# First layer of a two-layer block in float32 on one core: the norm's factor applied after the products instead of before them

## The reference, cut to what matters

```python
def rmsnorm(x, g):
    xf = x.astype(jnp.float32)
    y = xf * lax.rsqrt(jnp.mean(xf * xf, axis=-1, keepdims=True) + RMS_EPS)
    return (y * g.astype(jnp.float32)).astype(x.dtype)

h = rmsnorm(x, norm_mix_pre[l])
proj = h @ w_in[l]
xr, yr, q, k, v, g_rnn, g_attn = jnp.split(proj, IN_OFFSETS, axis=-1)
xr = causal_depthwise_conv(xr, conv_w[l], conv_b[l])
xr = rg_lru(xr, positions, w_a, b_a, w_x, b_x, lam)
y_rnn = xr * jax.nn.gelu(yr)
q, k = rope(q, positions), rope(k, positions)
y_att = sliding_window_sink_attention(q, k, v, attn_sinks[l])
mix = sigmoid(g_rnn) * (y_rnn @ w_rnn_proj[l]) + sigmoid(g_attn) * (y_att @ w_attn_proj[l])
x = x + rmsnorm(mix @ w_out[l], norm_mix_post[l])
...   # an MLP, then a second layer with three kinds of attention and a larger MLP
```

## Time and profile before

| | |
|---|---|
| median of 3 runs | 2827.66 us (2826.63 to 2828.91) |
| the profiled execution | 2828.23 us |
| its span in the trace | 2826.4 us |
| PE busy | 2758.0 us, 98% of the span |
| DVE, ACT busy | 1948.1 us (69%), 1337.4 us (47%) |
| PE waits: for the sum of squares, at the start | 13.4 us |
| PE waits: for normalised tiles (L600) | 8.2 us, 7 times |
| PE waits: for ACT in RG (L740) | 3.3 us, once |

### The profile page before, as it was taken

One profiled execution on the slowest core, in us unless ns is written; L12 is line 12 of the kernel. 1 busy time (PEld: TensorE's weight loads), 2 busy tenths in 40 slices (PEclk: granted clock), 3 DMA queues, 4 the chain that ended last, 5 costly groups with the idle time before them and its releaser, 6 DMA issues.

```text
span 2826.4 us, 50296 instructions
## 1 busy us (share of the span) xinstructions
PE 2758.0 (98%) x16433; PEld 2407.7 (85%) x16433; DVE 1948.1 (69%) x3013; ACT 1337.4 (47%) x2135; POOL 109.7 (4%) x206
## 2 busy tenths in 40 slices
PE   7999999999999999999999999999999999999998
PEld 6888888888887888888888789788888888888887
DVE  7878867766657774457754654856788885688855
ACT  5655455554444443334444443644554444444443
POOL 0000000000010000000000010100110000000000
PEclk9999999999999999999999999999999999999999
DMA  4555544445553556666555354354445545555554
GB/s 174 179 178 176 194 152 154 156 167 185 188 193 126 186 179 229 206 202 213 204 193 195 147 195 152 132 180 143 155 164 188 183 175 196 193 185 186 184 174 163
DMA packets 83196, 503.32 MB, mean 178 GB/s; under 512 B 9685, under 2 KB 17925, under 8 KB 31515
## 3 DMA queue, kind: packets, MB, share of 16 engines
q1 hardware_dynamic: 79868, 491.04, 49.8%
q0 software_dynamic: 3120, 11.14, 1.4%
q10 hardware_dynamic: 144, 0.30, 0.0%
HBM read 500.29 MB, written 10.55 MB: 181 GB/s over the span
## 4 chain that ended last, share of the span: by engine, by line
PE 59%; DVE 5%; issue 3%; ACT 2%; DVEq 0%; ACTq 0%
PE PS L568 33%; PE PS L572 17%; ACT w L1125 1%; PE PS L688 1%; PE PS L689 1%; PE PS L690 1%; PE PS L583 1%; DVE tmp L1713 1%; DVE w L1702 1%; PE PS L585 1%; PE PS L584 1%; DVE tmp L2147 0%; PE PS L875 0%; DVE tmp L2146 0%; PE PS L715 0%
## 5 line engine op out<-in xcount | busy, mean ns | idle before, releaser
L1702 DVE TENSOR_TENSOR w<-w_raw,w 128x1024 fp32r<-128x1024 f32 (+1 forms) x964 | 1099.8, 1173 | 421.1 <-ACT w L1125 419.6
L1125 ACT ACTIVATE w<-w_raw 128x1024 fp32r<-128x1024 f32 (+1 forms) x964 | 942.0, 1009 | 388.9 <-PE PS L572 239.0
L568 PE MATMUL PS<-h,w 128*128 128x512 f32 x3008 | 766.9, 397 | 4.7 <-ACT w L1125 2.1
L568 PEld LDWEIGHTS PS<-h,w 128*128 128x128 f32 x3008 | 540.5, 188 | 120.0 <-issue 18.1
L568 PE MATMUL PS<-u,w 128*128 128x512 f32 x1728 | 442.0, 394 | 5.2 <-ACT w L1125 5.2
L572 PEld LDWEIGHTS PS<-h,w 128*128 128x128 f32 x3008 | 410.1, 190 | 30.1
L572 PE MATMUL PS<-h,w 128*128 128x256 f32 x3008 | 418.7, 282 | 0.0
L568 PEld LDWEIGHTS PS<-u,w 128*128 128x128 f32 x1728 | 308.9, 189 | 58.5 <-ACT w L1125 5.8
L568 PE MATMUL PS<-f,w 128*128 128x512 f32 x1408 | 354.5, 394 | 4.0 <-DVE x L2388 4.0
L568 PEld LDWEIGHTS PS<-f,w 128*128 128x128 f32 x1408 | 254.4, 190 | 49.8 <-DVE x L2388 4.2
L572 PEld LDWEIGHTS PS<-u,w 128*128 128x128 f32 x1728 | 241.5, 190 | 21.0
(11 more groups left out here) (326 smaller groups left out, 2608.7 us busy)
## 6 DMA issues: line engine op xcount, KB each, us to landing
w_raw<-in_w_FU SPq DMA_DIRECT2D x88, 1024.0 KB, 4.7
w_raw<-in_w_UP SPq DMA_DIRECT2D x64, 1024.0 KB, 4.8
w_raw<-in_w_DN SPq DMA_DIRECT2D x64, 1024.0 KB, 4.8
w_raw<-in_w_FD SPq DMA_DIRECT2D x64, 704.0 KB, 4.0
w_raw<-in_w_G SPq DMA_DIRECT2D x32, 1024.0 KB, 4.7
w_raw<-in_w_Q SPq DMA_DIRECT2D x18, 1024.0 KB, 4.7
w_raw<-in_w_X SPq DMA_DIRECT2D x16, 1024.0 KB, 4.8
w_raw<-in_w_Y SPq DMA_DIRECT2D x16, 1024.0 KB, 4.7
```

The source lines that it names most:

```text
L568: pe.matmul(PS[:, bank, :], w_hi[:, 2 * s + hf, k * P:(k + 1) * P], rhs[:, k0 + k].rearrange("p a b -> p (a b)"), start=start and k == 0, ...
L1125: act.activation(w_hi[:, 2 * s + hf, 0:n * P], w_raw[:, s, off * P:(off + n) * P], ACT.Copy)\
L1702: tt(w_lo[:, slot, 0:n * P], w_raw[:, s, off * P:(off + n) * P], w_hi[:, slot, 0:n * P].bitcast(F32), ALU.subtract).then_inc(lo_ready, 1)
```

## The change

The first layer's products no longer take the normalised activations. `h_hi`/`h_lo` are made from x times the gain (`raw_high` on ACT, `raw_lower` on DVE), as each slice of x lands. SP loads the first two slices of x, then both first units of weights, then the other two slices. The squares, their sum, the root and the reciprocal still happen, but later: PE sums them in the middle of unit 2 (`x_sums`), together with two products that give the same sums with tokens along the partitions (for V). The factor is kept in `rstd_x` and later `rstd_g`. It is multiplied

- in X into every merged tile: `merge_x` becomes a copy of the bank's upper half on ACT (`x_lower`), an addition on DVE (`join_halves`) and a product on DVE (`scale_x`), and only then comes `tap`. The taps 2, 1 and 0 of a tile are done in the body of the next unit;
- in Q into `cos` and `sin`, once;
- in Y into every tile (`y_lower`, `join_y`, `scale_y` in place of `merge_y`);
- in V by the scale operand of the copy on ACT;
- for the gates by 16 products of two tiles each in MR and MA (`scale_gates`).

ACT's bodies of phase X are written out instead of being a hardware loop.

```diff
             for name, n, subs in STREAM:
+                if name == "X":
+                    for s in range(2):
+                        sp.dma_start(w_raw[:, s, :], dram["w_X"][s]).then_inc(w_landed[s], 16)
+                    load_x(2)
+                    load_x(3)
+                    sp.wait_ge(lo_ready, 4 + 3)
+                    load(name, 1, n // 2, subs)
+                    continue
...
-            sum_features(0)
-            pe.wait_ge(hi_ready, 1)
-            keep_busy(10, w_hi[:, 0, 0:P], w_hi[:, 0, 0:2 * S])
-            product("X", 16, h2, ready=(h_ready, 4), joint=True)
+            def x_sums(i, s):
+                if isinstance(i, int) and s == 0:
+                    sum_features(0)
+
+            pe.wait_ge(raw_lo, 1)
+            keep_busy(12, h_hi[:, 0, 0:P], h2[:, 0].rearrange("p a b -> p (a b)"))
+            product("X", 16, h2, ready=(raw_lo, 0), mid=x_sums, joint=2)
...
+            raw_high(0)
+            raw_high(1)
+            first_weights_hi(0, 0)
+            x_square(0)
+            for s, hf in ((1, 0), (0, 1), (1, 1)):
+                first_weights_hi(s, hf)
+            raw_high(2)
+            raw_high(3)
+            for k in range(1, 4):
+                x_square(k)
...
-            def body(i, first=False):
+            def x_lower(c, s):
+                act.wait_ge(half_done, units_done(U0["X"] + c))
+                act.wait_ge(xr_ready, c + 1)
+                act.activation(tmp[s][:, 3:3 + S], PS[:, s, S:2 * S], ACT.Copy).then_inc(x_low, 1)
+
+            def tap(c, s):
+                act.wait_ge(x_scaled, c + 1)
...
+            def body(i):
                 for s in range(2):
                     c, pair = 2 * i + s, U0["X"] // 2 + i
-                    if not first or s:
-                        conv_hi(c - 1)
+                    x_lower(c, s)
                     half_hi(pair + 1, s, 0, SUB)
...
+                    tap(c, s)
                     half_hi(pair + 1, s, 1, SUB)
...
+                    conv_hi(c - 1)
...
+            half_hi(1, 0, 0, SUB)
+            x_lower(0, 0)
+            half_hi(1, 0, 1, SUB)
+            x_lower(1, 1)
+            half_hi(1, 1, 0, SUB)
+            deviation()
...
+            tap(0, 0)
+            half_hi(1, 1, 1, SUB)
+            tap(1, 1)
+            conv_hi(0)
+            for i in range(1, 8):
                 body(i)
...
+            def scale_x(c, s):
+                pad = tmp[s][:, 3:3 + S]
+                dve.wait_ge(acc_free, 2 + T0["X"] + c + 1)
+                tt(pad, pad, rstd_x[:], ALU.mult).then_inc(x_scaled, 1)
...
+                    join_halves(c, s)
+                    dve.wait_ge(tap_ready, c)
+                    tap2 = link.mark(stt(t2, pad[:, 2:2 + S], conv_w(c - 1, 2), t2, ALU.mult, ALU.add))
                     half_lo(pair + 1, s, 0, SUB)
...
+                    scale_x(c, s)
                     link.wait(tap2)
...
+                    tap1 = link.mark(stt(t2, pad[:, 1:1 + S], conv_w(c - 1, 1), t2, ALU.mult, ALU.add))
+                    conv_lo(c - 2)
                     half_lo(pair + 1, s, 1, SUB)
                     link.wait(tap1)
...
+                    stt(xr[:, c - 1, :], pad[:, 0:S], conv_w(c - 1, 0), t2, ALU.mult, ALU.add).then_inc(xr_ready, 1)
...
+            tt(cos[:], cos[:], rstd_x[:], ALU.mult)
+            link(tt(sin[:], sin[:], rstd_x[:], ALU.mult))
...
+            def scale_gates(p):
+                dve.wait_ge(acc_free, 2 + T0["MR"])
+                own = bass.ds(2 * p, 2)
+                tt(gates[:, own, :], gates[:, own, :], windows(rstd_g, 0, P, 0, [[0, 2], [1, S]]), ALU.mult)                    .then_inc(gate_scaled, 2)
```

More of the change, by code:

```diff
@@ L194, in program @@
         rstd2 = place("rstd2", [P, S], at=reg_k + 2 * KB)
+        rstd_x = place("rstd_x", [P, S], at=reg_k + KB)
+        rstd_g = place("rstd_g", [P, S], at=reg_k + 3 * KB)
         cos = place("cos", [P, S], at=reg_k + 2 * KB)
@@ L586, in half_unit, with first_pair @@
                 mm.then_inc(half_done, 1)
-            def first_pair(name, rhs, ready, norm):
+            def first_pair(name, rhs, ready, norm, n_hi=3):
                 u, pair = U0[name], [(0, 0), (1, 1)]
@@ L625, in first_pair, with product @@
                 mm.then_inc(half_done, 3)
-            def product(name, n, rhs, mid=None, peel=False, subs=SUB, ready=None, norm=None, first=0, wide=True, joint=False):
+            def product(name, n, rhs, mid=None, peel=False, subs=SUB, ready=None, norm=None, first=0, wide=True, joint=0):
                 n0, n1 = split_sizes(subs)
@@ L647, in product @@
                 if joint:
-                    first_pair(name, rhs, ready, norm)
+                    first_pair(name, rhs, ready, norm, n_hi=joint)
+                    if mid is not None:
+                        pair(1)
                 elif peel or ready:
                     pair(0)
-                with pe.Fori(1 if peel or ready else first, n // 2) as i:
+                with pe.Fori(1 + (joint and mid is not None) if peel or ready else first, n // 2) as i:
                     pair(i)
@@ L697, in sum_features @@
                     pe.matmul(PS[:, 7, 0:S], ones[:], sq_sum[:], start=True, stop=True).then_inc(sums_ready, 1)
+                    for th in range(2):
+                        mm = pe.matmul(PS[:, 6, th:th + 1], sq_sum[:, th * P:(th + 1) * P], ones[:, 0:1], start=True, stop=True)
+                    mm.then_inc(tok_sums, 1)
                     return
@@ L1288, in body @@
                         round_y(c - 2, s)
+                    if not first or s:
+                        y_lower(c - 1, 1 - s)
                     next_hi(U0["Y"] // 2 + i, s, n, 1)
@@ L1835, in body @@
-                    if not first or s:
-                        conv_lo(c - 1)
+                    scale_x(c, s)
                     link.wait(tap2)
-                    tap1 = link.mark(stt(t2, pad[:, 1:1 + S], w[1], t2, ALU.mult, ALU.add))
+                    tap1 = link.mark(stt(t2, pad[:, 1:1 + S], conv_w(c - 1, 1), t2, ALU.mult, ALU.add))
+                    conv_lo(c - 2)
                     half_lo(pair + 1, s, 1, SUB)
                     link.wait(tap1)
-                    stt(xr[:, c, :], pad[:, 0:S], w[0], t2, ALU.mult, ALU.add).then_inc(xr_ready, 1)
@@ L1843, in _ @@
-            link.begin(0, 4)
-            body(0, first=True)
-            with dve.Fori(1, 7) as i:
-                link.begin(i, 4)
-                body(i)
-            link.begin(7, 4)
-            body(7)
-            link.end(8)
+                    stt(xr[:, c - 1, :], pad[:, 0:S], conv_w(c - 1, 0), t2, ALU.mult, ALU.add).then_inc(xr_ready, 1)
+            join_halves(0, 0)
+            half_lo(1, 0, 0, SUB)
+            join_halves(1, 1)
+            half_lo(1, 0, 1, SUB)
+            half_lo(1, 1, 0, SUB)
@@ new lines, in _ @@
+            inverse_deviation(rstd_x[:])
+            scale_x(0, 0)
+            scale_x(1, 1)
+            half_lo(1, 1, 1, SUB)
+            dve.wait_ge(tok_std, 1)
+            dve.reciprocal(rstd_tok[:, 2:4], rstd_tok[:, 0:2]).then_inc(tok_ready, 1)
+            dve.wait_ge(tap_ready, 1)
+            link(stt(tmp[2][:, 0:S], tmp[0][:, 2:2 + S], conv_w(0, 2), tmp[2][:, 0:S], ALU.mult, ALU.add))
+            link(stt(tmp[2][:, 0:S], tmp[0][:, 1:1 + S], conv_w(0, 1), tmp[2][:, 0:S], ALU.mult, ALU.add))
@@ new lines, in _ @@
+            stt(xr[:, 0, :], tmp[0][:, 0:S], conv_w(0, 0), tmp[2][:, 0:S], ALU.mult, ALU.add).then_inc(xr_ready, 1)
+            link.flush()
+            with dve.Fori(1, 8) as i:
+                link.begin(i - 1, 4)
+                body(i)
+            link.end(7)
+            last_t = tmp[3][:, 0:S]
+            dve.wait_ge(tap_ready, NC_D)
+            tap2 = link.mark(stt(last_t, tmp[1][:, 2:2 + S], conv_w(15, 2), last_t, ALU.mult, ALU.add))
+            conv_lo(NC_D - 2)
+            link.wait(tap2)
@@ L1851, in _ @@
+            link(stt(last_t, tmp[1][:, 1:1 + S], conv_w(15, 1), last_t, ALU.mult, ALU.add))
+            stt(xr[:, 15, :], tmp[1][:, 0:S], conv_w(15, 0), last_t, ALU.mult, ALU.add).then_inc(xr_ready, 1)
+            link.flush()
             conv_lo(NC_D - 1)
@@ L1914, in rope @@
                 link(tt(tmp[3][:, 0:S], PS[:, 6 + s, 0:S], sin[:], ALU.mult))
+                if last:
+                    link(dve.tensor_copy(rstd_g[:], rstd_x[:]))
                 tt(out, tmp[2][:, 0:S], tmp[3][:, 0:S], ALU.add).then_inc(rope_done, 1)
@@ L2092, in body @@
                     c = 2 * i + s
+                    if s == 0 and not isinstance(i, int):
+                        scale_gates(8 + i)
                     next_lo(U0["MA"] // 2 + i, s, n)
```

159 lines of the change are left out of this document (96 added, 63 removed).

## The result

| | before | after |
|---|---|---|
| median (16 runs each, same chip) | 2827.82 us (2826.43 to 2829.26) | 2834.65 us (2829.43 to 2836.21) |
| ratio, 95% interval | | 1.0022 (1.0015 to 1.0030) |
| the profiled execution, its span | 2828.23, 2826.4 | 2835.49, 2833.4 |
| pair 0 ends | 37.1 | 26.0 |
| `conv_hi(0)` | 42.13 | 37.56 |

The change costs 6.8 us by the medians, against 7.1 forecast. That it is slower is clear of the noise; whether by more than the 0.2% that the forecast's chances were set on is not, since the interval begins at 0.15%. In the profiled execution nearly all of the loss, 6.7, is there when `gates` start. The page of the changed kernel answers to the earlier trace rows: PE has 8 us more of busy time in a span that is 7 us longer, a share of 98% in both, so the page alone doesn't tell where the time went.

What follows compares the result with a forecast made beforehand. PE is 98% busy, but in-order waits between ACT and DVE set phase X's end. Start -5.1, ring +15.7 and tail -3.5 make +7.1 on 2827.66: 2834.8 us, range 2830.0 to 2839.0 (own case 2832.5 to 2838.5).

Steps and rivals of the forecast that it cites:

- the 0.2% that the forecast's chances were set on: Whole time: 5.7 us can be told; slower means above 2833.3, chance 0.74; same 0.18; faster, below 2822.0, 0.08.
- The start: Up to `conv_hi(0)`: first pair ends 12.6 us earlier, later norm leaves 5.1, so 37.0 instead of 42.13.
- rival 3: Clock falls in X's gaps: 65 us more, 2900, chance 0.04; only in the pair's first halves: 1.5 to 2.8, 2837.
- The ring: Phase X, waits between ACT and DVE: 6.51 a unit, taken as 6.57, instead of 5.45; 14 units cost +15.7.
- The addend of 0.06 for the loops: Phase X, per unit: half of the 0.12 that the old ring took more over the phase; bounds 0 and 0.12.
- The tail: End of X, from `conv_hi(14)` to `gates`: 2.17 instead of 5.64, a gain of 3.5 us.
- The sum at `gates`: End of X: `gates` start at 131.2 instead of 124.03, 7.1 us later, and PE takes that over.
- The terms named for the upper end of the range: Added to the forecast time: 0.8 for the ring, 2.5 for the start, 2 for the rest; own range to 2838.5.
- The rest at 0: After X: late scalings in Q, Y, V and for the gates lie beside waits; cost 0, in Y at most 1.4.
- (1): Phase X: waits don't bind, PE paces X; `gates` at 116 to 118, 7 us early, 2820.8; chance 0.08.
- (2): Phase X: 6.3 a unit and `conv_hi(0)` a microsecond earlier give +2.3, 2830.0; chance 0.17 for 2822.0 to 2833.3.

Runs made afterwards that it cites:

- the second profile: The changed kernel, unchanged, run and profiled once more; 2834.75 us, ratio 1.0023 to the kernel before.
- E8: Changed kernel with all four slices of x loaded ahead of the two units of weights; 2838.62 us, ratio 1.0038 to the kernel before.
- E1: Changed kernel with `scale_x` moved ahead of the first `half_lo` on DVE in phase X; 2814.65 us, ratio 0.9960 to the kernel before.
- E2: Changed kernel with ACT's second half of the weights moved ahead of the tap in phase X; 2820.28 us, ratio 0.9977 to the kernel before.
- E6: Changed kernel plus one unread 256-column product on DVE per unit of X, just ahead of `scale_x`; 2838.12 us, ratio 1.0036 to the kernel before.
- E7: Changed kernel plus one unread 256-column product on DVE per unit of X, ahead of the second `half_lo`; 2833.23 us, ratio 1.0021 to the kernel before.
- E3: Changed kernel without the factor's products in Q's tables, in Y and for the gates; 2833.08 us, ratio 1.0023 to the kernel before.

## Why the prediction was right, step by step

- **The start.** Forecast: pair 0 ends at 24.5 and `conv_hi(0)` runs at 37.0. Measured: 26.0 and 37.56 with part of the pair at half clock, 24.7 and 36.30 without (the second profile). That 37.0 lies between the two is partly luck, of two errors: the case without half clock was taken, and the way from the pair's end to `conv_hi(0)` was taken 0.9 too long, 12.5 against 11.5 and 11.6. Some 0.6 of that is the sum over the features, taken as 1.2 from the 1.19 of the earlier trace rows; it took 0.60 (L723). For the half clock I had named 1.5 to 2.8 in rival 3; it cost 1.3, or 1.5 if both executions are counted from their first product (6.72 and 6.95). E8 shows what the order of the transfers gives.
- **The ring.** Forecast 6.51, taken as 6.57; measured 6.50 in each of 14 turns. The addend of 0.06 for the loops was not there: my lower bound was right. The links that the change put into it are shown by E1 (`scale_x` and the tap off the first half: 5.31), E2 (the second half off the tap's wait: 5.53) and E6 against E7; the copy's link, 0.27, was read from the timeline and not varied.
- **The tail.** Forecast 2.17 from `conv_hi(14)` to `gates`, measured 2.15.
- **The sum at `gates`.** Forecast 131.2; measured 130.74 and 129.49. The forecast of +7.1 there was thus 0.4 to 1.6 high. Most of the profiles with this start ran their pair at full clock, and for such an execution the loss at `gates` is 5.5 and not 6.7. So the median's closeness to 7.1 is in part luck, and hangs on what comes later: from `gates` to the end of the span are 2702.4 before, 2702.7 and 2703.1 in the two profiles of the changed kernel. Such differences are of the size that profiles of this kernel and its variants show without a change of work there, see below. The terms named for the upper end of the range, 0.8, 2.5 and 2, would give 2840.1 and not 2838.5; the result is far from either.
- **The rest at 0.** E3 shows it for the late scalings. In MR and MA, DVE's wait for PE fell from the 29.0 of the earlier trace rows to 24.2 and PE had no new wait:

```profile
DVE tmp L1780 <- PE PS L596: 24.2, 17, 2.1
```

In E3, without `scale_gates`, that wait is back at its old length: the products were paid for out of it.

```profile
DVE tmp L1780 <- PE PS L596: 29.0, 17, 2.1
```

- **The rivals.** (1) The ring doesn't bind: false. PE waits for ACT's weights 11 times in X, and longer in RG. E1 is, by an edit, the world of that rival, and it is better there than its 2820.8: `gates` at 112.41, not 116 to 118, since only 7.4 us lie between the end of PE's last X product, 104.97, and `gates`, and not 12. (2) A shorter ring: false at 6.50, though in the executions at full clock `conv_hi(0)` did come 0.7 earlier than forecast. (3) The clock in X: it stayed at 1.00 over 81.5 us, with gaps of 0.26 in most units. The half clock at the start, the milder part of this rival, is there in some executions.

The Trainium skill ("TensorE: Matmul & The Clock Gate", A second HAM failure mode: psum-queue depth-cycling) tells of a kernel whose clock swings when PE stands still shortly between groups; taken as a rule for this phase, it gives at most the price of rival 3, since a clock that swings is not low all the time. The window of X after the change has PE idle for 6.0 of 81.5 us in short gaps and the clock at 1.00, and E6, with its longer ring, 10.0 of 84.5 (38.50 to 123.00) and also 1.00: the measurement decides against such a rule here.

## What to carry to other kernels

When two in-order engines hand a tile back and forth once more than before, walk the ring by starts and ends before placing the new instruction: here the product of 0.34 us, with the tap that waits for it, made a unit 1.2 us longer through the instruction that it stood behind (6.50 against 5.31), and one more such product cost nothing where it stood beside a wait (E7). Put the instruction that the other engine waits for ahead of the long one that nobody wants yet. And look for the gain of a shorter start at the point where the phase ends, since a ring longer than the bound engine's unit eats it in a dozen turns.
